# Experts' outputs: gated rows added to sums in DRAM by an indirect transfer

## What is computed

```python
def swiglu(x, wg, wu, wd):
    return (jax.nn.silu(x @ wg) * (x @ wu)) @ wd

def moe_swiglu(x, w_router, wg, wu, wd):
    xt = x.reshape(-1, d)                                   # 256 tokens x 1024, over both groups
    logits = (xt @ w_router).astype(jnp.float32)
    top_v, top_i = lax.top_k(logits, TOP_K)                 # 2 of 8
    top_w = jax.nn.softmax(top_v, axis=-1)
    gate = jnp.sum(jax.nn.one_hot(top_i, N_EXPERTS) * top_w[..., None], axis=1)
    out = jnp.zeros_like(xt)
    for e in range(N_EXPERTS):
        out = out + gate[:, e:e + 1] * swiglu(xt, wg[e], wu[e], wd[e])   # hidden width 2816
```

## Time and profile before

| | us |
|---|---|
| median of 3 runs | 1571.34 |
| lowest and highest | 1568.8, 1571.56 |
| the profiled execution | 1572.71 |
| its span, first to last instruction | 1570.8 |
| PE busy in the span | 1487.5 (95%) |
| VectorE busy | 545.6 (35%) |
| ScalarE busy | 296.6 (19%) |
| PE in gate/up and down products of the experts (L1481, L1501) | 452.5 + 238.4 |

### The profile page before, as it was taken

How to read it: one execution, slowest core, us unless ns; L and a number is a source line. 1 busy time by engine, 2 the same in 40 slices (tenths; PEclk the granted TensorE clock), 3 DMA queues, 4 the chain that set the end, 5 groups by cost and what they waited for, 6 DMA issues and landing times.

```text
span 1570.8 us, 62378 instructions
## 1 busy us (share of the span) xinstructions
PE 1487.5 (95%) x27941; PEld 1323.2 (84%) x27941; DVE 545.6 (35%) x1413; ACT 296.6 (19%) x821; POOL 15.3 (1%) x30
## 2 busy tenths in 40 slices
PE   5999888999998999899987999999999999999997
PEld 3888476999645787788866998999999999999997
DVE  1463435766627343576853211010100101010102
ACT  2112422001102341344414101010101001010101
POOL 0100000000000000000000000000000000000000
PEclk9999999999998999999999999999999999999999
DMA  9722677444548044000132599999999999999995
GB/s 391 289 86 93 249 287 291 162 162 165 197 174 321 16 160 172 10 8 6 35 140 93 223 417 363 419 389 410 417 377 417 385 418 373 419 382 418 383 413 234
DMA packets 73183, 407.07 MB, mean 259 GB/s; under 512 B 10546, under 2 KB 10980, under 8 KB 36196
## 3 DMA queue, kind: packets, MB, share of 16 engines
q1 hardware_dynamic: 68752, 399.96, 64.4%
q10 hardware_dynamic: 3412, 2.93, 0.6%
q0 software_dynamic: 896, 2.36, 0.5%
HBM read 403.31 MB, written 1.92 MB: 258 GB/s over the span
## 4 chain that ended last, share of the span: by engine, by line
PE 48%; DVE 1%; ACT 1%; issue 0%; DVEq 0%
PE bank L1481 27%; PE bank L1501 13%; PE bank L659 2%; PE bank L1463 2%; PE bank L1447 1%; PE bank L1457 0%; PE bank L1563 0%; PE bank L724 0%; PE bank L1282 0%; PE bank L1534 0%; DVE w L2071 0%; DVE w L2710 0%; PE bank L1305 0%; PE bank L1417 0%; ACT o L1595 0%
## 5 line engine op out<-in xcount | busy, mean ns | idle before, releaser
L1481 PE MATMUL bank<-w,ring 128*64 128x86 f32 x11264 | 452.5, 237 | 1.8 <-issue 1.2
L1481 PEld LDWEIGHTS bank<-w,ring 128*64 128x64 f32 x11264 | 432.3, 136 | 10.5 <-issue 9.7
L1501 PE MATMUL bank<-w,ring 128*64 128x86 f32 x5632 | 238.4, 237 | 0.0
L2899 DVE TENSOR_TENSOR w<-w,bank 128x86 f32<-128x86 f32 x176 | 43.1, 245 | 551.7 <-PE bank L1481 544.3
L1501 PEld LDWEIGHTS bank<-w,ring 128*64 128x64 f32 x5632 | 220.7, 137 | 0.0
L1994 ACT ACTIVATE w<-bank 128x86 f32<-128x86 f32 x176 | 42.8, 243 | 573.2 <-PE bank L1481 573.2
L656 PE MATMUL bank<-w,ring 128*128 128x256 f32 x256 | 59.2, 394 | 4.2 <-DVE w L2489 3.6
L656 PEld LDWEIGHTS bank<-w,ring 128*128 128x128 f32 x256 | 50.5, 198 | 13.0 <-DVE w L2489 3.9
L659 PE MATMUL bank<-ring,w 128*128 128x256 f32 x256 | 55.9, 379 | 1.9 <-DVE w L2071 1.9
L659 PEld LDWEIGHTS bank<-ring,w 128*128 128x128 f32 x256 | 48.4, 190 | 8.6 <-DVE w L2071 2.1
L682 PE MATMUL bank<-ring,ct 128*32 128x256 f32 x768 | 47.8, 402 | 2.1 <-ACT ct L1592 2.1
(11 more groups left out here) (444 smaller groups left out, 1798.2 us busy)
## 6 DMA issues: line engine op xcount, KB each, us to landing
ring<-in_moe_gu SPq DMA_DIRECT2D x176, 1024.0 KB, 8.8
ring<-in_moe_w_down SPq DMA_DIRECT2D x176, 512.0 KB, 8.9
ring<-in_ada_w SPq DMA_DIRECT2D x48, 1024.0 KB, 5.1
ring<-in_ev_w_in SPq DMA_DIRECT2D x11, 1024.0 KB, 25.8
ring<-in_ffn_w_gate SPq DMA_DIRECT2D x11, 1024.0 KB, 7.8
ring<-in_ffn_w_up SPq DMA_DIRECT2D x11, 1024.0 KB, 5.4
ring<-in_ffn_w_down SPq DMA_DIRECT2D x11, 1024.0 KB, 6.4
ring<-in_ev_w_out SPq DMA_DIRECT2D x4, 1024.0 KB, 11.1
```

Of the source, the lines that this page charges most:

```text
L1481: ins = [mm(b[hp, 0:CAP], w[:, k, hp], XG[:, k, :], start=k == 0, stop=k == KC - 1, skip_group_check=True) for hp in HALVES]
L1501: ins = [mm(bank[4 + c // 4][hp, (c % 4) * CAP:(c % 4 + 1) * CAP], w[:, c * P + hp.start:c * P + hp.stop], HIDU[:, t % 2, :], start=t == 0 ...
L2899: v.tensor_tensor(HIDU[:, t % 2, :], SILU[:, t % 2, :], bank[2 + t % 2][:, 0:CAP], ALU.mult).then_inc(sem("hid"), 1)
```

## The change

A buffer `sums` in DRAM takes the place of the sums O on the chip: 256 rows of 1024 for the tokens, and behind them 86 more, one for each slot that is empty in a unit. VectorE zeroes O early in unit 0, and POOL stores these zeros to `sums`.

In unit u (1 to 7) ScalarE's copy to YG multiplies each slot's row by the gate of its token, and POOL then adds the 86 rows of YG, the outputs of unit u-1, to `sums` with one indirect transfer, whose row numbers stand in SLOT_ROW. The four scatter products and VectorE's four additions are gone from these units. Only the last unit's outputs are scattered and added on the chip as before; ahead of that POOL reads the sums back into O, after the last indirect transfer.

The row numbers and gates of the slots come from two small products `slots`: SEL against three columns (token number, 1, gate). They replace the two transposes of SEL in units 1 to 6, and in unit 0 they are new, before the gather, in place of the transposes after down 0. VectorE turns them into SLOT_ROW and SLOT_GATE (`slot_rows`: an empty slot gets a row behind the tokens') at block 11 of a unit, for unit 0 at its end. Unit 0 has a selection matrix of its own (SEL0).

New waits: PE before the products `slots` for ScalarE's copies (unit_yg, in the place of the one ahead of the scatter), and at a unit's end for SLOT_GATE (selt); ScalarE's copy for the indirect transfer before (rows_summed); `slot_rows` for the one of its own unit; POOL for YG and for the transfer before; the last additions for the sums' return.

```diff
+            token_rows = SUMS[0:NST * P, :].rearrange("(s p) n -> p s n", p=P)
+            pool.wait_ge(sem("o_zero"), 1)
+            pool.dma_start(token_rows, O[:, :, :]).then_inc(sem("rows_summed"), 16)
+            pool.dma_start(SUMS[NST * P:NST * P + CAP, :], O[0:CAP, 0, :]).then_inc(sem("rows_summed"), 16)
+            pool.wait_ge(sem("table"), 1)
+            units = pool.value_load(TBL[0:1, UNITS:UNITS + 1], min_val=NE, max_val=UNITS)
+            with pool.Fori(1, units) as u:
+                pool.wait_ge(sem("unit_yg"), u * 2)
+                pool.wait_ge(sem("rows_summed"), u * 16 + 16)
+                pool.sem_inc(sem("settled"), 1)
+                pool.indirect_dma_start(SUMS[:, :], bass.IndirectOffsetOnAxis(ap=SLOT_ROW[0:CAP, 0:1], axis=0),
+                                        YG[0:CAP, :], None, compute_op=ALU.add).then_inc(sem("rows_summed"), 16)
+            pool.wait_ge(sem("rows_summed"), units * 16 + 16)
+            pool.sem_inc(sem("settled"), 1)
+            pool.dma_start(O[:, :, :], token_rows).then_inc(sem("rows_summed"), 16)
...
-            def scatter(st, first, done):
-                for h in range(2):
-                    mm(bank[first + h][:, :], SELT[:, st, :], YG[0:CAP, h * 512:(h + 1) * 512],
-                       start=True, stop=True).then_inc(sem(done), 1)
+            def slots(b, sel, tokens):
+
+                for st in range(NST):
+                    ins = mm(b[0:CAP, 0:3], sel[:, st, :], tokens[:, st, :], start=st == 0, stop=st == 1)
+                ins.then_inc(sem("selt_done"), 1)
...
                 gate_up(0, once(moe_slot("gu", 0)), outputs_turned)
+                gate_up(1, once(moe_slot("gu", 1)))
+                down(0, f"slot{moe_slot('d', 0)}", once(moe_slot("d", 0)), u * HB + (FT + 1))
                 if later:
                     pe.wait_ge(sem("unit_yg"), u * 2)
-                    scatter(0, 4, "scattered")
-                    scatter(1, 6, "scattered")
-                gate_up(1, once(moe_slot("gu", 1)))
-                if later:
-                    pe.wait_ge(sem("unit_taken"), shifted_by(u, prev, 4, -2))
-                down(0, f"slot{moe_slot('d', 0)}", once(moe_slot("d", 0)), u * HB + (FT + 1))
-                if later:
-                    pe.wait_ge(sem("unit_taken"), u * 4)
-                    pe.sem_inc(sem("settled"), 1)
-                for st in range(NST):
-                    ins = tr(bank[6][0:CAP, st * P:(st + 1) * P], SEL[:, st, :], ident)
-                ins.then_inc(sem("selt_done"), 1)
+                if prev is not None:
+                    for st in range(NST):
+                        ins = tr(bank[6][0:CAP, st * P:(st + 1) * P], SEL[:, st, :], ident)
+                    ins.then_inc(sem("selt_done"), 1)
+                elif later:
+                    slots(bank[6], SEL, TOKENS)
...
-                    A(YG[0:CAP, h * 512:(h + 1) * 512], bank[6 + h][0:CAP, :], ACT.Copy).then_inc(sem("unit_yg"), 1)
+                    if h == 0:
+                        act.wait_ge(sem("rows_summed"), u * 16 + 16)
+                    A(YG[0:CAP, h * 512:(h + 1) * 512], bank[6 + h][0:CAP, :], ACT.Copy, scale=SLOT_GATE).then_inc(sem("unit_yg"), 1)
...
+            def slot_rows(u, b):
+
+                dve.wait_ge(sem("selt_done"), u + 1)
+                dve.wait_ge(sem("rows_summed"), rows_summed(u))
+                v.tensor_scalar(SLOT_AT, b[0:CAP, 1:2], CST[0:CAP, C_BASE + 1:C_BASE + 2], CST[0:CAP, C_BASE:C_BASE + 1],
+                                ALU.mult, ALU.add).then_inc(made("unit_chain"), 1)
...
+                v.tensor_copy(SLOT_ROW[0:CAP, :], SLOT_AT).then_inc(made("unit_chain"), 1)
+                dve.wait_ge(sem("unit_chain"), so_far("unit_chain"))
+                v.tensor_copy(SLOT_GATE, b[0:CAP, 2:3]).then_inc(sem("selt"), 1)
...
-                for st, h in ((0, 0), (0, 1), (1, 0), (1, 1)):
-                    dve.wait_ge(sem("scattered"), shifted_by(u, prev, 4, 2 * st + h - 3))
-                    o = O[:, st, h * 512:(h + 1) * 512]
-                    v.scalar_tensor_tensor(o, bank[4 + 2 * st + h][:, :], GT1[:, st:st + 1], o,
-                                           ALU.mult, ALU.add).then_inc(made("unit_taken"), 1)
-                    dve.wait_ge(sem("unit_taken"), so_far("unit_taken"))
```

More of the change, by code:

```diff
@@ L155 @@
 C_ID, C_TRI, C_BLK, C_COS, C_SIN, C_ONE, C_STRIP = 0, 128, 640, 768, 800, 832, 833
-NCST = C_STRIP + NE
+C_TOK = C_STRIP + NE
+C_BASE = C_TOK + NST
+NCST = C_BASE + 2
 def constants():
@@ L166, in constants @@
     c[:, C_STRIP:C_STRIP + NE] = row % 32 == np.arange(NE)[None, :]
+    c[:, C_TOK:C_TOK + NST] = row + P * np.arange(NST)[None, :]
+    c[:, C_BASE:C_BASE + 2] = (NST * P + row) * np.array([[1, -1]])
     c[:, C_TRI:C_TRI + P] = row < col
@@ L401, in program @@
         TBL = sb("tbl", [P, 16], I32)
+        SLOT_ROW = sb("slot_row", [P, 1], I32)
+        SUMS = t["sums"]
         SILU = W[5][:, 0:2 * CAP].rearrange("p (b n) -> p b n", b=2)
@@ L420, in program, with rows_summed @@
         SELT = ROUTE[0:CAP, 768:1024].rearrange("p (s n) -> p s n", s=NST)
+        SEL0 = ROUTE[:, 1024:1024 + NST * CAP].rearrange("p (s n) -> p s n", s=NST)
+        TOKENS0, TOKENS = (ROUTE[:, 1200 + 6 * n:1206 + 6 * n].rearrange("p (s n) -> p s n", s=NST) for n in range(2))
+        SLOT_AT, SLOT_GATE = ROUTE[0:CAP, 1212:1213], ROUTE[0:CAP, 1213:1214]
+        def rows_summed(u):
+            return u * 16 + 32
         def shifted_by(u, prev, k, c):
@@ L1441, in _, with gather @@
             ins.then_inc(sem("routed"), 1)
-            def gather():
+            def gather(sel):
                 for c in range(KC):
@@ L1447, in gather @@
                         ins = [mm(bank[6 + c // 4][hp, (c % 4) * CAP:(c % 4 + 1) * CAP],
-                                  HTM[:, st, c * P + hp.start:c * P + hp.stop], SEL[:, st, :],
+                                  HTM[:, st, c * P + hp.start:c * P + hp.stop], sel[:, st, :],
                                   start=st == 0 and c % 4 == 0, stop=st == 1, skip_group_check=True) for hp in HALVES]
@@ L1459, in turn_y @@
                         ins.then_inc(sem(done), 1)
-            def scatter(st, first, done):
-                for h in range(2):
-                    mm(bank[first + h][:, :], SELT[:, st, :], YG[0:CAP, h * 512:(h + 1) * 512],
-                       start=True, stop=True).then_inc(sem(done), 1)
+            def slots(b, sel, tokens):
+                for st in range(NST):
+                    ins = mm(b[0:CAP, 0:3], sel[:, st, :], tokens[:, st, :], start=st == 0, stop=st == 1)
+                ins.then_inc(sem("selt_done"), 1)
             pe.wait_ge(sem("sel"), 1)
-            gather()
+            gather(SEL0)
             due0 = list(walk.due)
@@ L1541, in unit @@
                              u * HB + i * ROWS + (FT + t))
-                pe.wait_ge(sem("selt"), u + 1)
+                if later:
+                    pe.wait_ge(sem("selt"), u + 1)
                 if prev is None:
                     pe.wait_ge(sem("sel"), u + 2)
-                    gather()
+                    if not later:
+                        slots(bank[0], SEL0, TOKENS0)
+                    gather(SEL)
                 down(HB - 1, "slot_last", u * 16 + 16, u * HB + (FT + HB))
             unit(0)
+            pe.wait_ge(sem("selt"), 1)
             pe.wait_ge(sem("table"), 1)
@@ L1998, in unit @@
                     act.wait_ge(sem("y_turned"), shifted_by(u, prev, 2, h - 1))
-                    A(YG[0:CAP, h * 512:(h + 1) * 512], bank[6 + h][0:CAP, :], ACT.Copy).then_inc(sem("unit_yg"), 1)
+                    if h == 0:
+                        act.wait_ge(sem("rows_summed"), u * 16 + 16)
+                    A(YG[0:CAP, h * 512:(h + 1) * 512], bank[6 + h][0:CAP, :], ACT.Copy, scale=SLOT_GATE).then_inc(sem("unit_yg"), 1)
                 silu(1, u * UT + (N_MOE + gate_taken(1)), u * HB + FT)
-                act.wait_ge(sem("selt_done"), u + 1)
-                A(SELT[:, :, :].rearrange("p s n -> p (s n)"), bank[6][0:CAP, 0:TW], ACT.Copy).then_inc(sem("selt"), 1)
+                if prev is not None:
+                    act.wait_ge(sem("selt_done"), u + 1)
+                    A(SELT[:, :, :].rearrange("p s n -> p (s n)"), bank[6][0:CAP, 0:TW], ACT.Copy).then_inc(sem("selt"), 1)
                 with act.Fori(0, LOOPS) as i:
@@ L2023, in _ @@
                 act.wait_ge(sem("last_turned"), h + 1)
+                if h == 0:
+                    act.wait_ge(sem("rows_summed"), rows_summed(last))
                 A(YG[0:CAP, h * 512:(h + 1) * 512], bank[6 + h][0:CAP, :], ACT.Copy).then_inc(sem("last_yg"), 1)
@@ L2822, in _ @@
             for st in range(NST):
[L2823 removed]
+                ins = v.tensor_scalar(SEL0[:, st, :], IOTA1, PLACE[:, st * NE:st * NE + 1], None, ALU.is_equal)
             ins.then_inc(made("sel"), 1)
@@ L2854, in first_units, with first_tokens @@
                 v.tensor_copy(TBLF[:, 0:NE], IOTA[:, 0:NE]).then_inc(made("dve_chain"), 1)
```

(34 more changed lines are left out.)

9 lines of the change are left out of this document (2 added, 7 removed).

## The result

| | us |
|---|---|
| before, median of 4 runs beside it | 1570.21 |
| changed, median of 4 runs | 1610.68 (1606.17 to 1613.77) |
| ratio, 95% interval | 1.026 (1.0236 to 1.0284) |
| profiled execution of the changed kernel, its span | 1606.17, 1604.3 |

The change makes the kernel about 40 us slower. The forecast was 9 us faster; the rival of the few engines had said 1600, and the range ended at 1602.

A forecast was written before the change was run, and what follows sets the result against it. PE and the DMA engines were both nearly full: PE gives up 24.7 us, 15.6 return as waits for tiles, 9.1 remain. From 1571.34 us that gave, 1.4 lower than the profiled execution's result, 1562.2; range 1547 to 1602.

The forecast's parts named there:

- the rival of the few engines: Indirect transfers: 43 rows on each of two DMA engines, 13.5 us there; 1600 us in all; chance 3 in 10.
- The bound: Experts: TensorE busy 95% of the span, DMA engines at 9 tenths; only 3.6 us a unit of DMA time to spare.
- PE's side: Units 1 to 7: scatter's 3.63 us goes, slot products add 0.1; PE's unit falls from 86.52 to 83.0 us.
- The waits that the change adds on PE, ScalarE and VectorE: Waits for unit_yg, selt and the earlier transfer in the experts: all met in time, costing nothing.
- DMA's side, the price of a row: Indirect transfers: a 4 KB row takes one engine 0.157 us a pass; two passes of six rows, 1.88 us.
- the forecast's own sum: Experts: period is DMA's 82.9 + 1.88 = 84.8 us, above PE's 83.0; time 1562.2 us.
- (2) Seven indirect transfers: DMA term for the 86 added rows a unit: six rows on the fullest engine, two passes, 1.88 us.
- the turn from gain to loss: Units 1 to 7: the gain is zero where a unit's transfer takes the fullest DMA engine 3.2 us.
- The rival had the loss alternate: Few engines: first unit's last gate/up tile about 12 us late, next pair loses 2 to 4; 7 us a unit on the mean.
- waits of 1 to 2 us leave the clock alone: TensorE in the experts: clock stays at the 2.4 GHz level, since waits like one of 0.91 us did not lower it.
- The place of the waits: PE waits 1 to 2 us for gate/up tiles at steps 19 to 21 of a unit, none at its start.
- The zeros: Unit 0: storing zeros for 256 and 86 rows takes the DMA engines 2.5 + 0.94 us, 3.45 in all.

The follow-up runs named there:

- the kernel without the transfer: Changed kernel with a store of 16 rows of 64 bytes in place of each indirect transfer; median 1549.29 us.
- the series with 87, 88, 89 and 96 rows: Changed kernel with that many rows per indirect transfer in place of 86, the extra ones to unread rows; medians 1579.02, 1560.39, 1707.97 and 1561.93 us.
- the plain rows: Changed kernel with its 86 rows written without the addition, each unit overwriting; median 1561.91 us, period 85.11 us.
- the kernel with the zeros early: Changed kernel with 88 rows and zeros copied to the sums from a DRAM input before the experts, not stored in unit 0; median 1560.64 us.

## Why the prediction was wrong

**The bound, and PE's side: right.** The experts run between two nearly full resources. PE's offer of 3.63 us a unit was measured by the kernel without the transfer, 82.78 us of period against 83.0 forecast. The waits that the change adds on PE, ScalarE and VectorE cost nothing, as said: none of unit_yg, selt or rows_summed shows.

**DMA's side, the price of a row: right.** Two passes, 2 x 0.157 us, were chosen without a row; the records say 0.327. The packets of the queues in 6 us of the transfer of unit 2 (1066 to 1072 us; q0 is POOL's), with their count, MB and share of 16 engines' time:

```profile
q1 hardware_dynamic: 459, 2.37, 95.0%
q0 software_dynamic: 21, 0.09, 7.2%
```

0.072 x 6 x 16 = 6.9 us for 21 packets of 4 KB are 0.33 us each. That the second pass is the reading of the sum is not shown: the POOL queue counts the same bytes without the addition (7.29 MB against 7.31). Where the rows are spread over all engines, the forecast's own sum holds: period 84.8 forecast and 84.46 measured, time 1562.2 and 1561.93. That the times agree this closely is in part luck: unit 0 lost its 1.8 us there (86.4 against 84.5) mostly to a wait that the sum did not have, and not to the zeros.

**The step that failed** is the choice in "(2) Seven indirect transfers": six rows on the fullest engine. There are 43: 14.1 us on each of two engines where the sum had 1.88 on the fullest, against the 3.2 us at which it put the turn from gain to loss. 86 x 0.33 = 28 us of engine time ended within 26 to 28 us of the issue while the engines also carried weights, so it is more than one engine; the packets in flight and the series with 87, 88, 89 and 96 rows give two. The text had weighed this as a rival at 3 in 10 with nothing in the trace to decide it. The Trainium skill (DMA: Bandwidth & Descriptors, "Why a DMA increments its semaphore by 16 and not by 1") has the rule of the largest divisor, and the measured exception that it names is for direct copies. The runs agree with the rule for indirect ones, and the exception should not have been stretched to them.

**The rival's size.** It was put at 3.5 us a unit over before, 1600 us; it was 4.75, and 7.3 in the last unit, 1610.7. The rival had the loss alternate, 12 us and then 2 to 4. It does not: the six periods are 90.0 to 92.5 us. They obey roughly 82.9 + x - 5.9, x being the time on the fullest engine: 91.1 for 86 rows (91.27 measured), 106.1 for 89 (105.98), 86.5 for 87 (87.34). I fitted the 5.9 us to the first two; for the third it was computed ahead and came out 0.8 too low, and the plain rows miss it by 1.3. That the 5.9 us are a lead of the spared engines, which ends where the ring holds no more tiles, fits the 7.5 us without a load in unit 2, but it was argued and not tried with a larger or smaller ring.

**Two terms were missing:** the lower clock behind a wait of 3.5 us, 1.5 us a unit, and the steps at the tiles' pace behind it. The prediction let waits of 1 to 2 us leave the clock alone, from a row of 0.91 us. The wait of 1.99 us in unit 0 of the kernel without the transfer did leave it at 1.00. But behind the 2.05 us in unit 7 of the changed kernel the products of a tile took 4.07 us instead of 2.39, at the lower level.

**The place of the waits** was wrong too, steps 19 to 21: here they lie at gate/up 7, some 21 us after the transfer is issued (the expectations call it step 4 or 5). With 96 rows the loss does come late in a unit as forecast, but as six to ten steps that are 0.2 us longer (units 3 to 5) and not as waits of 1 to 2 us.

**The zeros** were priced at 3.45 us in unit 0 with a wait of 2.0; taking them away gave 0.4 us back there and nothing that the median shows.

## What to carry to other kernels

An indirect DMA whose count of rows has no large divisor up to 16 sat on few engines in every case here, with the addition and without; pad the count to a multiple of 16 with rows that nobody reads, and look at the time to landing, which gives it away at once (27.8 us for 86 rows, 9.1 for 96). Where tiles wait for all DMA engines, do not price a transfer by its bytes alone: work out its time on the fullest engine, not its share of the total bandwidth. Before removing work from an engine, ask what the second fullest resource allows: of PE's 3.5 us a unit only some 2 arrived even with the best spread, since the DMA engines were full.

## What had not been expected of the hardware

Because of the tiny packets the POOL queue has 6480 packets with 86 rows, 11632 with 89 and 2336 with 96, for nearly the same bytes. POOL's own instruction takes 2.46 us for 86 added rows and 1.45 us for 96. It is also 1.45 us for 86 rows without the addition, which have as many tiny packets (of 4 bytes), so their number alone does not set it.

In every kernel of this series with the changed program PE has waits for nothing that the profile shows, 3.9 to 7.0 us in all against 1.2 before: one of 1.4 to 2.0 us some 20 us into unit 0, one to three around the loop's first pass, and in most of them two in unit 7, each in the first pass through a piece of code. Around the first of them, in the 5 us from 890 us of the kernel with the zeros early, one packet of instructions runs between full queues of weights:

```profile
q1 hardware_dynamic: 349, 1.85, 96.7%
q8 instruction: 1, 0.02, 1.2%
```

A fetch of code that stands behind weight tiles would explain it; that was argued from this coincidence and not tried.
